# Two transformer blocks on one core: expert results summed by adding scatters in place of stored and gathered at the end

## What is computed

```python
gate = p_grp * softmax(top_val)                  # 2 experts of 32 per token
ys = (silu(x[slot_tok] @ w_gate[e]) * (x[slot_tok] @ w_up[e])) @ w_down[e]
ys = ys * slot_gate[:, None]
out = zeros((T, D)).at[slot_tok].add(ys)         # each token gets two rows
x = x + out
return rmsnorm(x, final_norm_g)
```

## Time and profile before

| | |
|---|---|
| runs | 2024.51 us median of 3 (2023.34 to 2026.22) |
| span of the profiled execution | 2015.6 us |
| PE busy | 1816.0 us (90%) |
| DVE, ACT, POOL busy | 852.1, 436.7, 992.8 us |
| DMA | 346.00 MB, mean 172 GB/s |
| chain that ended last, by engine | PE 71%, DMA 14%, DVE 10%, ACT 3% |

### The profile page before, as it was taken

How to read it: one execution, slowest core, us unless ns; L and a number is a source line. 1 busy time by engine, 2 the same in 40 slices (tenths; PEclk the granted TensorE clock), 3 DMA queues, 4 the chain that set the end, 5 groups by cost and what they waited for, 6 DMA issues and landing times.

```text
span 2015.6 us, 27480 instructions
## 1 busy us (share of the span) xinstructions
PE 1816.0 (90%) x9716; PEld 1274.7 (63%) x9716; DVE 852.1 (42%) x1244; ACT 436.7 (22%) x809; POOL 992.8 (49%) x536
## 2 busy tenths in 40 slices
PE   5999999999999799999999979998968988869783
PEld 4888888887777577888888747765743333323331
DVE  5444434320253567544443389777341111111114
ACT  3111100100244432111110053552321111111112
POOL 5888887777544378888887623321211111101001
PEclk8999999999999999999999989989979988989886
DMA  3333372433211123333333212210589999999995
GB/s 128 94 96 102 94 273 94 143 95 95 72 56 52 41 84 94 94 94 97 101 107 99 77 54 73 65 61 21 206 311 357 378 404 406 413 415 407 410 398 205
DMA packets 56977, 346.00 MB, mean 172 GB/s; under 512 B 8474, under 2 KB 8858, under 8 KB 44896
## 3 DMA queue, kind: packets, MB, share of 16 engines
q1 hardware_dynamic: 44640, 315.12, 42.7%
q10 hardware_dynamic: 7968, 19.46, 2.6%
q0 software_dynamic: 4320, 10.78, 1.5%
HBM read 475.06 MB, written 19.66 MB: 245 GB/s over the span
## 4 chain that ended last, share of the span: by engine, by line
PE 71%; DMA 14%; DVE 10%; ACT 3%; issue 1%; POOL 1%; SPq 0%; DVEq 0%; ACTq 0%; POOLq 0%
PE bank L460 31%; PE bank L431 12%; DMA big<-w_up_in 10%; PE bank L1821 7%; PE bank L1320 4%; PE bank L694 4%; PE bank L1839 2%; DVE big L1046 2%; PE bank L479 2%; PE bank L1434 2%; DMA ring<-w_down_in 1%; PE bank L1847 1%; DMA state<-w_down_in 1%; PE bank L612 1%; PE bank L672 1%
## 5 line engine op out<-in xcount | busy, mean ns | idle before, releaser
L277 POOL TENSOR_TENSOR weights_hi_parts<-ring,ones 128x1024 fp32r<-128x1024 f32 (+1 forms) x176 | 356.6, 2026 | 293.8 <-PE bank L460 130.2
L279 POOL TENSOR_TENSOR ring_parts<-ring,weights_hi_parts 128x1024 fp32r<-128x1024 f32 (+1 forms) x176 | 474.0, 2693 | 13.8
L460 PE MATMUL bank<-attention_buffers_parts,weights_hi_parts 128*128 128x512 f32 x832 | 328.1, 394 | 22.6 <-POOL ring_parts L279 17.9
L460 PE MATMUL bank<-state_parts,weights_hi_parts 128*128 128x512 f32 x832 | 325.7, 391 | 0.0
L460 PE MATMUL bank<-attention_buffers_parts,ring_parts 128*128 128x512 f32 x832 | 325.4, 391 | 0.0
L1821 PE MATMUL bank<-big,work 128*32 128x512 f32 x1440 | 227.6, 676 | 51.3 <-DMA big<-w_up_in 51.2
L431 PE MATMUL bank<-big_parts,weights_hi_parts 128*128 128x512 f32 x704 | 216.9, 389 | 1.2 <-POOL ring_parts L279 1.2
L460 PEld LDWEIGHTS bank<-attention_buffers_parts,weights_hi_parts 128*128 128x128 f32 x832 | 157.4, 189 | 59.1 <-POOL ring_parts L279 17.9
L1921 POOL TENSOR_TENSOR small<-small 128x1 f32<-128x1 f32 x51 | 9.7, 190 | 371.5 <-DVE small L1744 371.5
L866 POOL TENSOR_TENSOR ring_parts<-ring,weights_hi_parts 128x1024 fp32r<-128x1024 f32 x32 | 80.7, 2524 | 220.2 <-ACT weights_hi_parts L863 220.2
L460 PEld LDWEIGHTS bank<-state_parts,weights_hi_parts 128*128 128x128 f32 x832 | 157.5, 189 | 32.9 <-issue 0.8
(11 more groups left out here) (386 smaller groups left out, 2830.2 us busy)
## 6 DMA issues: line engine op xcount, KB each, us to landing
big<-w_up_in SPq DMA_DIRECT2D x54, 2048.0 KB
ring<-wdense_in SPq DMA_DIRECT2D x176, 512.0 KB, 3.6
state<-w_down_in SPq DMA_DIRECT2D x37, 2048.0 KB
big<-w_gate_in SPq DMA_DIRECT2D x36, 2048.0 KB
attention_buffers<-w_gate_in SPq DMA_DIRECT2D x18, 2048.0 KB
ring<-w_down_in SPq DMA_DIRECT2D x18, 2048.0 KB
ring<-wff_in SPq DMA_DIRECT2D x32, 704.0 KB, 4.1
y_rows<-big ACTq DMA_DIRECT2D x1, 8192.0 KB, 28.1
```

The lines of the kernel that those rows point to most:

```text
L277: po.tensor_tensor(hi, raw, ones[:, 0:1].to_broadcast([128, words]), ALU.mult).then_inc(PO.sem, 1)
L279: po.tensor_tensor(lo, raw, hi.bitcast(F32), ALU.subtract) \
L460: m = pe.matmul(out, x, y_, start=j + n == 0, stop=j == len(pairs) - 1 and n == len(ts) - 1)
```

## The change

The results are no longer stored block by block and gathered at the end. `y_rows` becomes `summed_results`, with two rows of 512 per token and two more for padding. The gates are spread over the table of blocks and applied as a scale when ACT copies the first products (to the "up" half alone, as `row_scale` is 1 for the others); so the second products come out weighted. POOL adds each block's result to its tokens' rows with an indirect transfer (`scatter_step`), which waits for the one before it. Rows out of range are skipped; of an empty block partitions 0 and 32 go to the padding rows. At the end four adding loads put the sums on top of `x_tok`, and DVE's multiply-adds are gone. POOL's loop runs one lap less, and its last two laps' scatters stand behind it. ACT's stores are gone. The table of tokens is now made for 64 partitions, and the one-hot tables lie in other buffers.

```diff
-Y_ROWS = -(-MAX_BLOCKS * BS // 128) * 128
+HALF_ROWS = 2 * T + 2
...
-    zeros = big[:, 44 * T:44 * T + D]
+    zeros = big[:, 44 * T:44 * T + 512]
     cleared = PO.run(po.memset(zeros, 0.0))
+    po.dma_start(y_d[2 * T:2 * T + 2, :], zeros[0:2, :]).then_inc(s_y, 16)
...
-        numbered = PO.run(po.tensor_scalar(tok_id[:, t:t + 1], tok_id[:, 0:1], float(t % NT * 128), None, ALU.add))
+        PO.run(po.tensor_scalar(tok_id[:, t:t + 1], tok_id[:, 0:1], float(t % NT * 128), None, ALU.add))
+    PO.run(po.tensor_tensor(not_up, ident[:, 0:1], ident[:, 32:33], ALU.add))
+    PO.run(po.tensor_scalar(half_row, tok_id[:, 0:1], float(BS - NO_ROW), None, ALU.is_ge))
+    PO.run(po.tensor_scalar(last_row, not_up, -1e6, 1e6 + 2 * T, ALU.mult, ALU.add))
+    PO.run(po.tensor_tensor(last_row, last_row, half_row, ALU.add))
+    PO.run(po.tensor_scalar(is_up, tok_id[:, 0:1], float(3 * BS - NO_ROW), None, ALU.is_ge))
+    PO.run(po.tensor_scalar(not_up, tok_id[:, 0:1], float(2 * BS - NO_ROW), None, ALU.is_ge))
+    PO.run(po.tensor_tensor(is_up, is_up, half_row, ALU.add))
+    PO.run(po.tensor_tensor(is_up, is_up, not_up, ALU.subtract))
+    PO.run(po.tensor_scalar(not_up, is_up, -1.0, 1.0, ALU.mult, ALU.add))
+    numbered = PO.run(po.tensor_scalar(half_row, half_row, float(2 * NO_ROW), None, ALU.add))
...
-            ac.dma_start(y_d.rearrange("(n p) c -> p n c", p=128),
-                         zeros.unsqueeze(1).to_broadcast([128, Y_ROWS // 128, D])).then_inc(s_fill, 16)
+            ac.dma_start(y_d[0:2 * T, :].rearrange("(n p) c -> p n c", p=128),
+                         zeros.unsqueeze(1).to_broadcast([128, 2 * NT, 512])).then_inc(s_fill, 16)
...
+    DV.step(dv.tensor_scalar(all_but_two.bitcast(I32), turn, -2.0, None, ALU.add))
...
-    s = PE.step(product(banks[2][0:BS, 0:SLOT_COLS],
-                        [(oh_row[:, c * BS:(c + 1) * BS], oh_tok[:, c * SLOT_COLS:(c + 1) * SLOT_COLS])
-                         for c in range(C2)]))
+    def by_rows(bank, cols_, table, copies):
+        for c in range(C2):
+            for g in range(copies):
+                m = pe.matmul(bank[g * BS:(g + 1) * BS, cols_], oh_row[:, c * BS:(c + 1) * BS],
+                              table[:, c * SLOT_COLS:(c + 1) * SLOT_COLS], start=c == 0, stop=c == C2 - 1,
+                              tile_position=(0, g * BS))
+        return m
+    s = PE.step(by_rows(banks[2], slice(0, SLOT_COLS), oh_tok, 2))
...
-    for q in (PE, AC, PO, DV):
+    PO.wait(counted_laps)
+    laps["po"] = po.value_load(all_but_two[0:1, 0:1].bitcast(I32), min_val=lo - 1, max_val=hi - 1)
+    for q in (PE, AC, DV):
...
-    DV.run(dv.scalar_tensor_tensor(posf, place, float(BS), rmod, ALU.mult, ALU.add))
-    DV.run(dv.tensor_copy(pos.bitcast(I32), posf))
+    row_at, added_to = sm(SLOT_COLS)[0:2 * BS, :], sm(SLOT_COLS)[0:2 * BS, :]
+    DV.run(dv.tensor_scalar(row_at, banks[2][0:2 * BS, 0:SLOT_COLS], 2.0, half_row[0:2 * BS, :], ALU.mult, ALU.add))
+    DV.step(dv.tensor_scalar(added_to.bitcast(I32), row_at, last_row[0:2 * BS, :], None, ALU.min))
...
+    gated_slots = DV.run(dv.tensor_tensor(by_slot(oh_gate), by_slot(oh_slot), over_last(gates, C2, SLOT_COLS), ALU.mult))
...
+    row_scale = sm(SLOT_COLS)
+    dv.wait_ge(s_spread, 1)
+    dv.tensor_scalar(row_scale, banks[7][:, 0:SLOT_COLS], is_up, not_up, ALU.mult, ALU.add).then_inc(DV.sem, 3)
...
-        ac.activation(gu, first_products[c % SETS][:, :], ACT.Copy).then_inc(AC.sem, 1)
+        ac.activation(gu, first_products[c % SETS][:, :], ACT.Copy,
+                      scale=row_scale[:, bass.ds(i * SETS + c, 1)]).then_inc(AC.sem, 1)
...
-    def act_store(i, c):
-        ac.wait_ge(DV.sem, at_step(DV, DV_Y, i, c + 1))
-        store(i, c)
-    def store(i, c):
-        for half in range(2):
-            ac.dma_start(y_d[bass.ds(i * (SETS * BS) + c * BS, BS), half * 512:half * 512 + 512],
-                         y_e[c % SETS][half * BS:(half + 1) * BS, :]).then_inc(s_y[c % SETS], 16)
-    def dve_result(i, c, steps=1):
+    def dve_result(i, c, steps=1, scattered=None):
+        dv.wait_ge(PO.sem, i * (2 * SETS) + (pool_begun + (2 * c if scattered is None else scattered)))
+        dv.tensor_copy(to[c % SETS].bitcast(I32), added_to[:, bass.ds(i * SETS + c, 1)].bitcast(I32)).then_inc(DV.sem, 1)
...
-        dv.wait_ge(s_y[c % SETS], i * 32 + (32 * (c // SETS) + 16))
...
-    gathers_begun = PO.n
+    def gather_step(i, c, n):
+        po.wait_ge(PO.sem, i * (2 * SETS) + (pool_begun + n))
+        po.wait_ge(DV.sem, at_step(DV, DV_IDX, i, c - 1))
+        po.tensor_tensor(zo, zc, zc, ALU.add).then_inc(PO.sem, 1)
+        gather(c % SETS, idx[c % SETS][0:BS, :])
+    def scatter_step(i, c, n, summed=DV_Y):
+        b = c % SETS
+        po.wait_ge(PO.sem, i * (2 * SETS) + (pool_begun + n))
+        po.wait_ge(DV.sem, at_step(DV, summed, i, c + 1))
+        po.wait_ge(s_y, i * (16 * SETS) + (16 * c + 16))
+        po.tensor_tensor(zo, zc, zc, ALU.add).then_inc(PO.sem, 1)
+        po.indirect_dma_start(y_d[:, :], bass.IndirectOffsetOnAxis(ap=to[b].bitcast(U32), axis=0), y_e[b], None,
+                              bounds_check=2 * T + 1, oob_is_err=False, compute_op=ALU.add).then_inc(s_y, 16)
+    po.wait_ge(s_fill, 16)
+    gather_step(0, 0, 0)
+    gather_step(0, 1, 1)
     with po.Fori(0, laps["po"]) as i:
         for c in range(SETS):
-            po.wait_ge(PO.sem, i * SETS + (gathers_begun + c))
-            po.wait_ge(DV.sem, at_step(DV, DV_IDX, i, c - 1))
-            po.tensor_tensor(zo, zc, zc, ALU.add).then_inc(PO.sem, 1)
-            gather(c, idx[c][0:BS, :])
+            gather_step(i, c + 2, 2 * c + 2)
+            scatter_step(i, c, 2 * c + 3)
+    before_last = laps["po"]
+    gather_step(before_last, 2, 2)
+    for c in range(2 * SETS - 1):
+        scatter_step(before_last, c, c + 3)
+    scatter_step(before_last, 2 * SETS - 1, 2 * SETS + 2, DV_IDX)
+    ac.wait_ge(DV.sem, at_step(DV, DV_MUL, 0, -1))
...
+    PE.wait(gated_slots)
+    by_rows(banks[7], slice(0, SLOT_COLS), oh_gate, 4).then_inc(s_spread, 1)
...
-    for b in range(SETS):
-        po.wait_ge(s_y[b], laps["po"] * 32 + 48)
-    po.wait_ge(PO.sem, laps["po"] * SETS + gathers_begun)
+    po.wait_ge(s_y, before_last * (16 * SETS) + (16 * 2 * SETS + 16))
+    po.wait_ge(PO.sem, before_last * (2 * SETS) + (pool_begun + 2 * SETS + 3))
     po.tensor_tensor(zo, zc, zc, ALU.add)
-    picked = [[big[:, (2 * t + j) * D:(2 * t + j + 1) * D] for j in range(2)] for t in range(NT)]
+    summed = y_d[0:2 * T, :].rearrange("(t h) c -> t (h c)", h=2)
...
     for t in range(NT):
-        for j in range(2):
-            c = j * NT + t
-            po.indirect_dma_start(picked[t][j], None, y_d[:, :],
-                                  bass.IndirectOffsetOnAxis(ap=pos[:, c:c + 1].bitcast(U32), axis=0)).then_inc(s_pick[t], 16)
+        po.dma_start(x_tok[:, t * D:(t + 1) * D], summed[t * 128:(t + 1) * 128, :], accum_op=ALU.add).then_inc(s_pick[t], 16)
...
-            xt = x_tok[:, t * D:(t + 1) * D]
-            dv.wait_ge(s_pick[t], 32)
-            for j in range(2):
-                s = DE.run(dv.scalar_tensor_tensor(xt, picked[t][j], gates[:, j * NT + t:j * NT + t + 1], xt, ALU.mult, ALU.add))
...
-            AE.wait(s)
-            squares.append(AE.step(ac.activation(nrm[:, t * D:(t + 1) * D], xt, ACT.Square, accum_out=st[:, t:t + 1])))
+            ac.wait_ge(s_pick[t], 16)
+            squares.append(AE.step(ac.activation(nrm[:, t * D:(t + 1) * D], x_tok[:, t * D:(t + 1) * D], ACT.Square,
+                                                 accum_out=st[:, t:t + 1])))
```

More of the change, by code:

```diff
@@ L144, in build @@
     s_wexp = [[sem(f"expert_weights_{n}_{b}") for b in range(SETS)] for n in ("gate", "up", "down")]
-    s_y = [sem(f"block_results_stored_{b}") for b in range(SETS)]
-    s_fill = sem("block_results_cleared")
-    s_pick = [sem(f"results_gathered_{t}") for t in range(NT)]
+    s_y = sem("block_results_added")
+    s_fill, s_spread = sem("summed_results_cleared"), sem("gates_spread")
+    s_pick = [sem(f"results_summed_{t}") for t in range(NT)]
     s_out = sem("output_stored")
@@ L171, in build @@
     hi_raw, weights_hi = sb2("weights_hi", 2 * SLOT)
-    sumsq, rinv = sb("sum_of_squares", T), sb("token_scale", T)
+    both_scales = sb("sum_of_squares_and_token_scale", 2 * T)
+    sumsq, rinv = both_scales[:, 0:T], both_scales[:, T:2 * T]
     banks = [nc.alloc_psum_tensor(f"bank{i}", [128, 512], F32) for i in range(8)]
@@ L191, in sm @@
         return small[:, a:a + n]
+    h_d = nc.dram_tensor("h_rows", (T, D), F32).ap()
+    y_d = nc.dram_tensor("summed_results", (HALF_ROWS, 512), F32).ap()
     wr, zc, zo, minus_half, dummy = sm(KD * 36), sm(1), sm(1), sm(1), sm(1)
@@ L556, in build @@
     dv.wait_ge(s_fill, 16)
+    dv.wait_ge(s_y, 16)
     section(3, at["qk"] + RING, wdense_d, KD * 128, lambda i: qk_group(i, RING * T), 4, 0, 4)
@@ L1634, in build @@
     heads, ids1, key, ahead = sm(3), sm(C2), sm(33), sm(1)
```

(37 more changed lines are left out.)

13 lines of the change are left out of this document (6 added, 7 removed).

## The result

The changed kernel takes **2028.03 us** (median of 11 runs, 2025.06 to 2031.93); the kernel before, run beside it on the same chip, 2022.60 (11 runs, 2021.60 to 2026.22). The ratio is 1.0023, 95% interval [1.0014, 1.0031]: 0.23% slower. Run again beside further runs of before, it gave 2030.46 against 2024.02, 1.0032 [1.0020, 1.0045]. The forecast was 2019.6 and faster. The range held the time, the direction was wrong.

The account below looks back on a forecast made before the run. The expert stage's long stretch was taken as bound by transfers, with nothing overlapping at the end. Terms +1.7 - 1.4 + 0 - 5.2 = -4.9 us gave a span of 2010.7 and a median of 2019.6 us; range 2010 to 2044.

Parts of the forecast that it names:

- Before the first block: Ahead of the first expert block: doubled token-table product, lap count and gates' spread cost +1.7 us (0 to +4.5).
- The 0.5 allowed for it: First block: the gates' spread delays it 2.3 us, mostly hidden by a queued load's wait; 0.5 us, between 0 and 2.3.
- The clearing and POOL's start: Kernel start and clearing of y: POOL's ten small instructions cost nothing (uncovered 3.7 us), the smaller clearing gains nothing.
- The bytes in the loop: Bound stretch: adds of 3.03 MB replace stores of 5.12 MB, -1.4 us (-5.1 to +2.3).
- k = 2: Loop and end: an adding transfer costs two copies, if reads limit; upper bound, sum +1.8 us, 2026.3 us.
- k = 1.5: Loop and end: an adding transfer costs 1.5 copies, accesses counted; the value taken for the forecast.
- k = 1: Loop and end: an adding transfer costs the same as a copy; lower bound, sum -11.5 us, 2013.0 us.
- The chain of scatters: Loop, POOL: each scatter awaits the one before; landing 8.2 us, period 9.0 under 9.36, so covered narrowly: 0 us.
- The end: After the last result: four adding loads replace gathers and multiply-adds, -5.2 us (-8.1 to -2.2).
- the fixed part: Final loads: 4.1 us were taken as fixed, and 5.9 us as moved bytes that the adding cost multiplies.
- Adds move at half a copy's rate: Rival, loop and end: adds cost two copies, sum +1.8 us, 2026.3 us, no change that can be told; chance 0.20.
- The chain as the bound: Rival, POOL's wait for the previous scatter: landings from about 9 us slow the loop, 2038 us, up to 2060; chance 0.31.

Follow-up runs that it names:

- experiment 5: The changed kernel with the gates' spread multiplied ahead of the wait for the first gather, not behind the first block's products: 2028.47 us, 1.0031.
- experiment 3: The changed kernel with scatters that overwrite and don't add, same chain of waits, leaving out the sum over a token's two experts: 2016.11 us, 0.9963.
- experiment 7: The changed kernel with a row per assignment, unchained copying scatters, no clearing, eight plain loads and DVE's additions at the end: 2021.56 us, 0.9988.
- experiment 10: The changed kernel with empty rows added too, to spare rows, so each scatter adds 64 rows: 2032.10 us, 1.0040.

## Why the prediction was wrong

**Before the first block (+1.7, 0 to 4.5).** The doubled product of the token table is free. Its piece in the chain, against the 2.01 us of 16 records in the earlier trace rows:

```profile
1491.55 2.02 PE bank L1725 x32
```

The spread stands in the chain as foreseen, with VectorE's 0.36 us and ACT's 0.70 behind it:

```profile
1499.80 5.81 PE bank L1847 x32
1505.61 1.00 PE bank L1725 x55
...
1506.71 0.36 DVE small L1816
1507.09 0.70 ACT weights_hi L1879
...
1513.26 21.86 DMA big<-w_up_in
```

It runs into the same long wait for a load, and taking it off this path (experiment 5) changed nothing. The 0.5 allowed for it was not too small.

**The clearing and POOL's start (0).** POOL's timeline at the start, the first and the last of the ten small instructions and the operation behind them:

```profile
8.33 0.19 POOL L232 TENSOR_TENSOR small<-ident 128x1 f32<-128x1 f32 x1
...
12.89 0.73 POOL L241 TENSOR_SCALAR small<-small 128x1 f32<-128x1 f32 x1
13.71 1.89 POOL L292 TENSOR_TENSOR weights_hi_parts<-ring,ones 128x1024 fp32r<-128x1024 f32 x1
```

The ten take 5.3 us where 2.8 was the estimate, since some take 0.7; the pause covers them but for 0.7 us (12.99 in the earlier trace rows). No run isolates that. The clearing moves less at no gain, as PE is as busy as in the earlier trace rows:

```profile
270.00:305.00 35.00, 35.00 (x155) 28.95 (x155) 14.67 (x8) 3.13 (x5) 28.18 (x10) 1.00 0.49 163
```

**The bytes in the loop (-1.4; -5.1 to +2.3).** This is the step that failed. It measured +7 to +12 (502.7 and 505.9 against 494.3 and 495.6), beyond even its bound for k = 2. It failed twice. First, the choice of k = 1.5, "accesses counted": k is 2.0 in two doses, and 1.9 at the end. With k = 2 the term was +2.3, so this is the smaller part of the miss. Second, the reckoning by bytes. With k = 1 the step from 5.12 MB to 3.03 was to give back 5.1 us. The stores took 3.9% of the engines' time and copying scatters take 2.4%: 1.5 points less, 5.5 us of the stretch. Yet experiment 3's loop is only 1.6 to 2.9 us shorter than before's, and with experiment 7's 495.5 nothing is gained. The adding is paid in full, 9.1 us of 365; the saved bytes are given back by half at most.

The queues of the changed kernel say where the loss sits. It moves 8.6 us less of weights in the stretch. The other queues take 1.0 point more (6.5% to 7.5%), 3.7 us; the sum of the shares is 0.7 points lower (100.8% to 100.1%), 2.6 us, mostly the gap at 1850. The remaining 2.3 us are in the weights' own packets, which carry less per share (141.55 MB for 94.3%, 138.20 for 92.6%): those of 16 KB take 636 ns before and 640 after. In experiment 3 they take 642, and the weights' queue 95.3% for the same 141.64 MB. That is 1.0 of the 1.5 points that the stores gave back; the other 0.5 stays unused (100.8% to 100.3%). A reckoning by bytes sees neither.

**The chain of scatters (0).** Right. The landing was 8.7 for 8.2, the period 9.0 to 9.2 for 9.0, and in the loop the cover held, narrow as it was: unchaining gained nothing there. In part that may be the loss's own doing, as blocks that wait longer for weights give the chain its time. With all rows added (experiment 10) the cover is all but gone.

**The end (-5.2, -8.1 to -2.2).** Right: 32.2 and 32.1 us before, 26.7 and 27.1 after. The chain of waits, from the last scatter to the last landing:

```profile
2001.09 3.12 DMA summed_results<-ring,small
...
2006.57 11.95 DMA big<-summed_results
```

The last scatter lands 6.5 us after the last result's start (forecast 1990.4 less 1983.35, 7.1). The last load lands at 2018.52, 20.8 us after that start, exactly where it was forecast (2004.1 less 1983.35). In between the loads took 13.7 us where 12.9 stood, and the last scatter landed earlier. With k = 2 they were to take 15.9: the fixed part was put too high, as 13.7 less 4 x 2.8 is 2.5, not 4.1. Two errors, k too low and the fixed part too high, nearly cancelled here; only the first went into the loop.

**The rivals.** "Adds move at half a copy's rate" named the mechanism, and 2026.3 is the nearest of the forecasts to 2028.0; it had 0.20 of the chance and should have been the forecast. It is the rule of the Trainium skill that was weighed there ("Collectives: The Full Stack", "The bandwidth ceiling: the fold count and why AG ≠ RS ≠ AR"): two source reads, half of a copy's rate. The runs agree with the half rate, 4.9% against 2.4% and 7.3% against 3.7% of the engines; that two reads are the reason, no run here shows. The chain as the bound, at 0.31, had the sign but not the cause.

**What stays open.** Which engines lag beside the adds, and why; why a packet of weights takes longer beside scatters than beside stores; and how much of the loop each of these is worth.

## What to carry to other kernels

An add in the transfer cost the DMA engines about two copies here. Where they are the bound, as in a stream of weights, copy each contribution to its own row and add at the end on a compute engine. Here that is 0.3 to 0.4% faster than the changed kernel, and 0.1% faster than the kernel before (experiment 7). Even where the queues are quiet, a plain load of a sum that began with the residual is 5 us cheaper for 2 MB than an adding one. Don't credit skipped rows with their bytes at the stream's rate: here they gave back half at most.

## What the runs showed of the hardware

- An adding transfer takes twice the engine time of a copying one per byte (4.9% to 2.4%, 7.3% to 3.7%). A row of 2 KB takes 180 ns added, a packet of 4 KB 178 ns copied, a stored one of 2 KB 86 ns. At the end a packet of 4 KB takes 352 ns added and 190 copied.
- Skipped rows leave packets of 8 bytes that take a DMA engine 9 ns each (948 in the stretch for 39 scatters, changed kernel; none where all rows are written).
- A packet of 16 KB of weights takes 636 ns beside stores and gathers (before), 642 beside copying scatters (experiment 3).
- POOL is busy 1.41 us issuing an adding scatter of 64 rows, 0.93 for a copying one (the 39 of each above).
- A gather on the same queue lands in 8.5 us beside adding scatters, 6.8 before.
- Skipping 41% of the rows of a scatter gained nothing that can be told in the kernel's time when it copies (2016.11 skipped, 2015.54 all rows), and 1.6 to 4.1 us when it adds (2030.46 and 2028.03 skipped, 2032.10 all rows). Beside skipping adds the last part of a weights' load came 3.2 to 4.3 us behind the median one, 2.4 with all rows added and 2.3 to 2.5 before.
- The same code starts the expert stage almost 5 us apart in two executions (1489.1 and 1493.75 before), as much as the change cost (0.23% of 2022.6 is 4.7).
